# RWKV-7 head norm made by ACT chunk by chunk inside the state loop, and the output projection's first slices loaded one block earlier

## The reference, cut to what matters

```python
def step(S, inp):                       # the state, here in chunks of 128 tokens
    sa = einsum('bhvk,bhk->bhv', S, a_t)
    S = S * w_t + sa[..., None] * b_t + v_t[..., None] * k_t
    return S, einsum('bhvk,bhk->bhv', S, r_t)          # y
mu = mean(y, axis=-1)                                   # over the 64 channels of a head
var = mean(square(y - mu), axis=-1)
y = ((y - mu) * rsqrt(var + 64e-5)).reshape(b, T, W) * ln_w + ln_b
out = (y + bonus) * silu(z_d)
mixed = concatenate([s5_out, out], axis=-1)             # 1024 columns: 512 of the S5 branch, 512 of RWKV
return x + mixed @ w_out
```

## Time and profile before

| | us |
|---|---|
| median of 3 runs | 1537.95 |
| lowest, highest | 1529.24, 1540.2 |
| the profiled execution | 1530.25 |
| span of its instructions | 1528.4 |

### The profile page before, as it was taken

The page is one execution under the profiler, slowest core; times in us unless marked ns, Lnnn a source line. Parts: engine busy times, 40 slices in busy tenths (PEclk is TensorE's granted clock), DMA queues, the critical chain, the costliest instruction groups (busy, mean ns, idle before and its releaser), DMA issues. The chain is left out here.

```text
span 1528.4 us, 20526 instructions
## 1 busy us (share of the span) xinstructions
PE 1319.8 (86%) x8434; PEld 1103.1 (72%) x8434; DVE 893.7 (58%) x1191; ACT 480.3 (31%) x822; POOL 307.5 (20%) x156
## 2 busy tenths in 40 slices
PE   4999999899779969959997999998334799999698
PEld 4677888678569848858886888885122698889587
DVE  5277754930257664159975665843888758265841
ACT  5233244222346651132421122312553211212310
POOL 2232211211023362032211111221301300000320
PEclk9999999989889979979999999999665557799899
DMA  5212112320300042232331425221000000010523
GB/s 183 43 42 66 31 46 70 96 70 15 138 22 2 2 138 83 96 76 90 99 97 52 121 64 176 52 83 56 0 1 1 1 1 1 2 56 2 193 82 112
DMA packets 117558, 97.79 MB, mean 64 GB/s; under 512 B 37016, under 2 KB 102680, under 8 KB 117336
## 3 DMA queue, kind: packets, MB, share of 16 engines
q1 hardware_dynamic: 103832, 77.45, 17.1%
q10 hardware_dynamic: 13632, 19.01, 3.8%
HBM read 70.23 MB, written 24.51 MB: 62 GB/s over the span
## 5 line engine op out<-in xcount | busy, mean ns | idle before, releaser
L167 PE MATMUL banks<-xt_lo,w_hi 128*128 128x512 f32 x816 | 323.2, 396 | 6.2 <-POOL w_lo L497 6.2
L168 PE MATMUL banks<-xt_hi,w_lo 128*128 128x512 f32 x816 | 319.9, 392 | 0.0
L169 PE MATMUL banks<-xt_hi,w_hi 128*128 128x512 f32 x816 | 319.6, 392 | 0.0
L497 POOL TENSOR_TENSOR w_lo<-features,w_hi 128x1024 fp32r<-128x1024 f32 x55 | 148.9, 2708 | 529.5 <-ACT w_hi L506 529.5
L167 PEld LDWEIGHTS banks<-xt_lo,w_hi 128*128 128x128 f32 x816 | 154.6, 189 | 42.1 <-POOL w_lo L497 6.7
L169 PEld LDWEIGHTS banks<-xt_hi,w_hi 128*128 128x128 f32 x816 | 154.5, 189 | 32.7
L168 PEld LDWEIGHTS banks<-xt_hi,w_lo 128*128 128x128 f32 x816 | 154.5, 189 | 31.2
L550 ACT ACTIVATE temporaries<-banks 128x1024 f32<-128x1024 f32 x47 | 56.1, 1193 | 328.5 <-PE banks L169 319.8
L506 ACT ACTIVATE w_hi<-features 128x1024 fp32r<-128x1024 f32 x55 | 57.8, 1055 | 27.9 <-PE banks L169 26.7
L295 PE MATMUL banks<-temporaries,features 128*128 128x128 f32 x256 | 38.3, 314 | 27.5 <-DVE temporaries L272 27.5
L167 PE MATMUL banks<-xt_lo,oout_mh 128*128 128x512 f32 x128 | 51.1, 399 | 11.9 <-DVE xt_lo L1581 11.9
(11 more groups left out here) (449 smaller groups left out, 2601.2 us busy)
## 6 DMA issues: line engine op xcount, KB each, us to landing
features<-in_even_w_in SPq DMA_DIRECT2D x26, 512.0 KB, 4.0
features<-in_odd_w_in SPq DMA_DIRECT2D x25, 512.0 KB, 4.3
features<-in_x SPq DMA_DIRECT2D x8, 512.0 KB, 8.6
even_gates<-temporaries ACTq DMA_DIRECT2D x8, 512.0 KB, 2.6
features<-even_gates SPq DMA_DIRECT2D x8, 512.0 KB, 8.1
features<-in_even_w_out SPq DMA_DIRECT2D x8, 512.0 KB, 3.5
temporaries<-in_x SPq DMA_DIRECT2D x8, 512.0 KB, 4.6
h_between_layers<-features SPq DMA_DIRECT2D x8, 512.0 KB, 3.1
```

Source lines behind the costliest of these rows:

```text
L167: nc.tensor.matmul(out, w[0], x[1], start=start, stop=False)
L168: nc.tensor.matmul(out, w[1], x[0], start=False, stop=False)
L169: return nc.tensor.matmul(out, w[0], x[0], start=False, stop=stop)
L497: nc.gpsimd.tensor_tensor(wl[n % 2], wr[n % NW], wh[n % 2].bitcast(F32), ALU.subtract).then_inc(low, 1)
```

## The change

In `r7_state`, after each chunk's y, ACT makes four copies out of PSUM, one for each head, each with a sum over its 64 channels; then the negated mean, four squares of y minus the mean with their sums, and the root, all for 4 columns of statistics. DVE inverts the root and forms minus mean times inverse one chunk later, behind its R copy, and ACT then writes the normal rows over y in four instructions with scale and bias (due 10 c + 5.5). The last chunk's come at due 80. This holds for both state blocks. In exchange `r7_finish` begins with the transposes: its six passes on DVE, the small scaling, and its root on ACT are gone. Its due numbers in the second state block go from 5 + 3.4 t to 8 + 6 t.

In `project_out` of the odd layer the first two slices (weights and S5 activations, four loads of 512 KB) are loaded in the second state block, behind the gates on SP's queue, into the places of half 0's k and v. The high parts lie elsewhere, so that slices 4 to 7 overwrite those places: ACT waits for four low parts of either kind ahead of slice 4. The order in the last block begins with slice 0's split, and the products of slice 0 stand between the two sets of transposes. `x.mean`, `x.var` and `x.rs` now lie in separate places for each half. In the diff, cut to its core, the parts are those of `project_out`, `r7_state`, `gates_of`, `r7_finish` and `odd_layer`, in this order; of `r7_finish` only the due numbers are shown.

```diff
-    wr = [co.at(A_F[4] + 1024 * i, (D,)) for i in range(3)]
+    ahead = [] if w_ahead is None else w_ahead
+    wr = ahead + [co.at(A_F[4] + 1024 * (k % 3), (D,)) for k in range(KT - len(ahead))]
+    L = len(ahead)
...
-        for k in range(3):
-            if not fetched:
-                sp.dma_start(wr[k], w[k * P:(k + 1) * P, :]).then_inc(loaded[k], 16)
+        for k in range(L, L + 3):
+            if L or not fetched:
+                sp.dma_start(wr[k], w[k * P:(k + 1) * P, :]).then_inc(loaded[k % 3], 16)
...
     def scalar(act):
         for k in range(KT):
-            yield 5 + 2.5 * k if k < early else base + k
+            yield (0, 3, 5, 7)[k] if k < early < KT else base + k
             if k < len(fetch):
                 act.wait_ge(mixed_in[k], 16)
             if k == early:
                 act.wait_ge(*ready)
+                act.wait_ge(low_m, early)
+                act.wait_ge(low_w, early)
...
     def gpsimd(pool):
-            yield 5 + 2.5 * k if k < early else base + k
+            yield k if k < early else base + k
...
     def tensor(pe):
-            yield 8 + 3.5 * k if k < early else base + 2 + k
+            yield (1, 5.5, 6, 7)[k] if k < early < KT else base + 2 + k
...
     def vector(dve):
-            yield (6, 9.5, 11, 15.5)[k] if k < early < KT else base + k
+            yield (0, 3.5, 5, 8.5)[k] if k < early < KT else base + k
...
-                pe.wait_ge(y_out, c)
+                pe.wait_ge(y_out, 4 * c)
+        def inverse(c):
+            dve.wait_ge(rooted, c + 1)
+            nc.vector.reciprocal(x.rs[:, own(c)], x.rs[:, own(c)]).then_inc(inverted, 1)
+            dve.wait_ge(inverted, 2 * c + 1)
+            nc.vector.tensor_tensor(x.mean[:, own(c)], x.mean[:, own(c)], x.rs[:, own(c)], ALU.mult).then_inc(inverted, 1)
...
             nc.vector.tensor_copy(R, read).then_inc(r_out, 1)
+            if c:
+                inverse(c - 1)
...
+        yield 10 * NT
+        inverse(NT - 1)
+        def normal(c):
+            act.wait_ge(inverted, 2 * c + 2)
+            for j, cols, i in heads:
+                at = slice(4 * c + i, 4 * c + i + 1)
+                nc.scalar.activation(rows(c, j, cols), rows(c, j, cols), ACT.Identity, bias=x.mean[:, at], scale=x.rs[:, at]).then_inc(normed, 1)
...
                 take(c + 1, 1)
+            if c:
+                yield 10 * c + 5.5
+                normal(c - 1)
             yield 10 * c + 8
             act.wait_ge(ys, c + 1)
-            nc.scalar.activation(x.kk[:, :, c * P:(c + 1) * P], out, ACT.Copy).then_inc(y_out, 1)
+            for j, cols, i in heads:
+                nc.scalar.activation(rows(c, j, cols), out[:, j, cols], ACT.Copy, accum_out=x.var[:, 4 * c + i:4 * c + i + 1]).then_inc(y_out, 1)
+            act.wait_ge(y_out, 4 * c + 4)
+            nc.scalar.activation(x.mean[:, own(c)], x.var[:, own(c)], ACT.Copy, scale=-1.0 / 64).then_inc(centred, 1)
+            act.wait_ge(centred, c + 1)
+            for j, cols, i in heads:
+                nc.scalar.activation(square[:, i, :], rows(c, j, cols), ACT.Square, bias=x.mean[:, 4 * c + i:4 * c + i + 1], accum_out=x.var[:, 4 * c + i:4 * c + i + 1]).then_inc(squared, 1)
+            act.wait_ge(squared, 4 * c + 4)
+            nc.scalar.activation(x.rs[:, own(c)], x.var[:, own(c)], ACT.Sqrt, bias=co.at(co.eps_at[GN_EPS], (1,)), scale=1.0 / 64).then_inc(rooted, 1)
+        yield 10 * NT
+        normal(NT - 1)
+        for to, what, sem in ahead:
+            sp.dma_start(to, what).then_inc(sem, 16)
         sp.wait_ge(gates_in, 16 * 4)
-            yield pace(13 + 4 * j)
+            yield pace(3 + 4 * j)
...
-            yield pace(12.4 + 4 * j)
+            yield pace(2.4 + 4 * j)
...
-            yield pace(10 + 5 * j)
-            pe.wait_ge(normed, 1)
+            yield pace(5 * j)
+    w_in, mixed_in = [co.sem(f"oout_w{i}", kept=True) for i in range(3)], [co.sem(f"oout_mixed{i}", kept=True) for i in range(2)]
+    mixed_at, w_at = [co.at(A_F[i], (T,)) for i in (3, 2)], [co.at(A_F[i] + 1024, (D,)) for i in (3, 2)]
+    ahead = [load for i in range(2) for load in ((w_at[i], a["odd_w_out"][0][i * P:(i + 1) * P, :], w_in[i]), (mixed_at[i], oc[i], mixed_in[i]))]
+    high_at = [A_F[2] + 2048, A_F[2] + 3072, A_F[3] + 2048, A_F[3] + 3072, A_F[2], A_F[2] + 1024, A_F[3], A_F[3] + 1024]
...
-    side_by_side(co, clearing(co), gates_of(co, zg), r7_state(co, second), r7_finish(co, first, (co.gates_in, 64), A_BIG, 0, lambda t: 5 + 3.4 * t))
+    side_by_side(co, clearing(co), gates_of(co, zg, ahead), r7_state(co, second), r7_finish(co, first, (co.gates_in, 64), A_BIG, 0, lambda t: 8 + 6 * t))
```

More of the change, by code:

```diff
@@ L1474, in swa_attend, with project_out @@
     return dict(sync=sync, gpsimd=gpsimd, tensor=tensor, vector=vector, scalar=scalar)
-def project_out(co, tag, w, mixed, hi_at, lo_at, res, dst, stored, fetched=False, fetch=(), early=KT, ready=None, keep=None):
+def project_out(co, tag, w, mixed, hi_at, lo_at, res, dst, stored, fetched=False, fetch=(), early=KT, ready=None, keep=None, w_ahead=None, fetched_mix=()):
     nc = co.nc
@@ L1511, in sync @@
             sp.dma_start(rr[k], res[k * P:(k + 1) * P, :]).then_inc(resin[k], 16)
-        for k in range(3, KT):
+        for k in range(L + 3, KT):
             sp.wait_ge(low_w, k - 2)
-            sp.dma_start(wr[k % 3], w[k * P:(k + 1) * P, :]).then_inc(loaded[k % 3], 16)
+            sp.dma_start(wr[k], w[k * P:(k + 1) * P, :]).then_inc(loaded[k % 3], 16)
         for t in range(NT):
@@ L2123, in __init__ @@
         self.n_st = co.at(A_BIG + 4096 * half, (NT * 4, P))
+        self.mean, self.var, self.rs = (co.at(m + (864 if half else 680) + 32 * i, (32,)) for i in range(3))
         self.blocks = co.at(R7_INVERT[half]["blocks"], (NT * 4, 32))
@@ L2380, in r7_state @@
     S, R, SA = (co.at(A_T + 1536 + 256 * i, (2, P)) for i in range(3))
-    zeroed, turned, tok_out, pairs_made, kept, rs, r_out, solved, sa_out, ys, y_out, grown, added, updated = (
-        co.sem(f"r7s{half}_{y}") for y in ("zeroed", "turned", "tok_out", "pairs_made", "kept", "rs", "r_out", "solved", "sa_out", "ys", "y_out", "grown", "added", "updated"))
+    zeroed, turned, tok_out, pairs_made, kept, rs, r_out, solved, sa_out, ys, y_out, grown, added, updated, centred, squared, rooted, inverted, normed = (
+        co.sem(f"r7s{half}_{y}") for y in ("zeroed", "turned", "tok_out", "pairs_made", "kept", "rs", "r_out", "solved", "sa_out", "ys", "y_out", "grown", "added", "updated",
+                                           "centred", "squared", "rooted", "inverted", "normed"))
+    square = co.at(A_BIG + 12288, (4, 64))
+    heads = [(j, slice(64 * h, 64 * h + 64), 2 * j + h) for j in range(2) for h in range(2)]
+    own = lambda c: slice(4 * c, 4 * c + 4)
+    rows = lambda c, j, cols: x.kk[:, j, c * P + cols.start:c * P + cols.stop]
     both = lambda b: co.ps[:, b, 0:2 * P].rearrange("p (j t) -> p j t", j=2)
@@ L2544, in r7_finish @@
     half = x.half
-    y = x.kk.rearrange("p j (g v) -> p (j g) v", v=64)
-    sq = co.at(at, (32, 64))
-    yt = [co.at(at + 2048 + 1024 * j, (T,)) for j in range(2)]
-    mean, var, rs = (co.at(A_MISC + 680 + 32 * i, (32,)) for i in range(3))
+    yt = [co.at(at + 1024 * j, (T,)) for j in range(2)]
     ident = co.at(A_CST + C_ID, (P,))
-    summed, rooted, normed, turned, mapped, done, dch = (co.sem(f"r7n{half}_{y_}") for y_ in ("summed", "rooted", "normed", "turned", "mapped", "done", "dch"))
+    turned, mapped, done, dch = (co.sem(f"r7n{half}_{y_}") for y_ in ("turned", "mapped", "done", "dch"))
     c_ = lambda n, j: x.cols[n][:, x.b0 + j:x.b0 + j + 1]
```

33 lines of the change are left out of this document (9 added, 24 removed).

## The result

The change makes the kernel slower by 0.8%: 1543.56 us (median of 13 executions, 1537.14 to 1550.5) beside 1532.89 (13 executions of the kernel before, 1522.34 to 1540.2), ratio 1.0076 with a 95% interval of 1.0052 to 1.0100. The profiled execution took 1542.1 us, its span 1540.3. The forecast was 1544 us.

What follows compares the result with a forecast made beforehand. TensorE's own instructions were taken to bound the second state block. First state block +10.5, second -0.5, last -2.25 make +7.75 on 1530.25 us, 1538; +6 for the clock gives 1544 us, range 1527 to 1561.

Steps and rivals of the forecast that it cites:

- Statistics per chunk: ACT's new copies, mean, squares and root in each chunk take 3.15 us from the y copy's start, bounds 2.5 and 4.0.
- (a): First state block, 1308.73: statistics come ahead of the inversion's L817 copies, where TensorE already waits 0.40 us; +2.76 us.
- (b): First state block, 1324.29: statistics come ahead of L817, where TensorE already waits 1.29 us; +2.76 us.
- (c): End of the first state block: last statistics, DVE's pair and normal rows precede L817; the block ends 2.6 us later.
- (d): First state block, 1265.8 to 1282.9, DVE busy: its wait for the root holds back its pass at 1270.05; +1.9 us.
- (e): First state block: one earlier set of normal rows stands ahead of an L817 pair; +0.45 us, an estimate.
- Second state block: ACT's statistics cost 0.5 us over seven chunks, DVE's removed passes give 1.0; net -0.5 us, bounds -1 and +2.
- Last block: Starts 4.8 us later, first product 5.0 us after its start instead of 10.75; net -2.25 us, bounds -5 and +1.
- Clock at the joint: After a 2.75 us rest the second state block begins at half clock for 13.6 us x 0.45; +6 us.
- The rule on engines: The skill puts multiplications and additions on VectorE; ACT's 10 us of normal rows were judged free wherever ACT idles.
- Rival (1): The clock holds at the joint of the state blocks: 1538 us; chance 0.2.
- Rival (4): First state block's half-clock stretches move by luck, up to 20 us less at half, -9 us: 1529; chance 0.07.

Runs made afterwards that it cites:

- e4: The change with mean, squares, root and normal rows due behind L817 in the first state block alone; ratio 1.0025 to the kernel before.
- e1: The change with statistics for the second half alone, half 0's single y copy and six DVE passes restored; ratio 1.0052 to the kernel before.
- e5: The change with four more unread fp32 products of 128x512 on TensorE around the inversion's last step, at the joint; ratio 1.0023 to the kernel before.
- e8: e1 with DVE's inverse of the root behind its second mask and the normal rows 2 us later; ratio 0.9971 to the kernel before.
- e9: e8 with e6's five filling products ahead of the first state block; ratio over all executions 0.9912 to the kernel before.
- e6: The kernel before with five more unread fp32 products of 128x512 in TensorE's rest ahead of the first state block; ratio 0.9941 to the kernel before.
- e11: e9 with five more filling products in TensorE's rest ahead of the last block; ratio over all executions 0.9873 to the kernel before.
- e2: The change's early loading and splitting of slices 0 and 1 alone, without statistics in either state block; ratio 1.0011 to the kernel before.
- e10: e8 without the early loading and splitting of the output projection's first two slices; ratio 1.0030 to the kernel before.
- e12: The kernel of e8 measured once more, unchanged; ratio 1.0027 to the kernel before.

## Why the prediction was right

Total and sign were right, and the mechanism too: +12.3 us in the mean span, of which the fit gives 7.3 to the clock of the whole program (forecast +6, for the joint alone) and 5.0 to the rest (forecast +7.75; the profile's blocks without the clock: 11.1 less 0.5, less 3.3 in the last block, +7.3). That the total was met within half a microsecond is luck in part: the forecast added 13.75 us to an execution of 1530.25 us, 2.6 below the median of 13, while the medians lie 10.7 us apart. Its +0.4% came out as +0.8%, because the three executions known then had a median 5 us above that of thirteen. By its steps:

- **Statistics per chunk, 3.15 us**: 2.98. The copies out of PSUM were cheaper than set (0.20 us each with their read, not 0.33), the squares as set (0.33). Normal rows 1.43 (1.3), from the root's end to the rows 0.45 (0.45).
- **(a), (b) and (c), L817 behind statistics**: shown, waits of 2.97, 3.86 and 2.49 us where 3.16, 4.05 and a block 2.6 us longer were forecast. e4 shows the cause: with the statistics behind L817, all waits for it are 2.6 us.
- **(d) DVE's stretch, +1.9**: wrong. DVE did wait for the root, 1.12 us in that stretch, and TensorE waited 1.24 us for the masks behind it; but the wait of 1.41 us of before is gone in return, and over the block TensorE's waits for DVE didn't grow (3.7 us, before 3.9).
- **(e) one earlier set of normal rows, +0.45**: mis-sized. Four normal rows and a turn's copy stand ahead of L817 at 1296.63, and TensorE waited 3.71 us where before it had no such wait. With DVE's passes shifted as well, the rows' 1.43 us are only part of it. (d) and (e) erred in opposite directions, 1.9 too much and 3.3 too little; the sum of the five, 10.5, met 11.1.
- **Second state block, -0.5**: idle time 2.1 to 1.6 us. That ACT's work fits behind TensorE there holds only in the order chosen: in e1's profile the same instructions went with 2.7 us more idle time, because DVE's pair then stood ahead of a long pass.
- **Last block, -2.25**: -3.3. The first product came 4.7 us after the block's start (5.0), the two low parts one behind the other, as priced (GpSimd's 2.35 us, forecast 2.6; DVE's ended 1.08 us behind it, forecast 1.3).
- **Clock at the joint, 13.6 us x 0.45**: it fell as said, for 17.1 us; in the second block it cost 4.9 us (4.4 longer with 0.5 less idle). e5 shows that filling the rests around the joint goes with a full start. The forecast judged by the size of the rest (a fall behind 1.29 and 1.41 us, none behind 1.04). That didn't carry: at the same rest of 1.04 us the clock held in the kernel before, e8 and e9 and fell in e6 and e11, and in e1, e2, e10 and e12 it was at half already when the joint came.
- **The rule on engines**: the text weighed the Trainium skill ("ScalarE: Activation LUTs", section "Rules for kernel authors"), by which such arithmetic belongs on VectorE, against free time on ACT. ACT's 31.5 us more in the first state block cost TensorE 11 us in one order and 5 in another (e4: 11.8 us idle against 6.8). The rule's outcome, a loss, came true here, mostly for a reason of order. The rule itself wasn't tested: no run gives the normal rows to DVE chunk by chunk, though a DVE pass over 128x2048 takes 2.28 us when GpSimd is idle (L2612 in e1), not the 4.49 that the text set against ACT.

Rival (1), clock holds, is the state of e5, at 3.6 us over before (forecast 7.75). Rival (4), luck, is real in size: e8 and e12 differ by 6.8 us in the mean as the same kernel, on two chips.

## What to carry to other kernels

Work put on an engine with idle time costs what stands behind it in that engine's order: look for the next instruction that the bounding engine waits for, and put the new work behind it (e4). A small instruction that waits for another engine should not stand ahead of a long pass or a mask that TensorE waits for (e8). Where rests move the clock, judge a change of under 1% by time at half clock and by idle time as well, since the total alone gave two answers for one kernel (e8 and e12).

## What the runs showed of the hardware

- TensorE stayed at 0.50 for 51.1 us while busy for 50.3 us of them, with small products (1215.1 to 1266.2 us of the kernel before); with five products of 128x512 ahead of it the block began at 1.00 and the fall came 27 us later (e6). A rest of 1.04 us at the same place went with a fall in two executions (e6, e11) and with none in three others (before, e8, e9).
- A microsecond at half clock went with 0.37 us more span over 271 executions; by issued products the forecast had taken 0.45.
- ACT's accumulate pairs follow one another every 0.20 us (128x64 copy out of PSUM) or 0.33 us (square with bias, from SBUF); the read of 0.19 us overlaps its neighbours.
- The one table load of ACT in the state block (L2556, 1236.19) took 1.28 us, and the next ACT instruction began 0.01 us behind it; TensorE, at half clock there, had no wait.
- A DVE product of two SBUF inputs of 128x1024 took 1.22 us with GpSimd idle and 3.32 us beside GpSimd's (e2).
- Two groups of times, 1507 to 1511 and 1529 to 1538 us, for one kernel (e9; e11 is alike, e6 less clearly). What picks the group isn't settled.
